# DeltaNet encoder kernel, opening of the first layer: gate products between the turns of the input, one convolution ahead of running sums, block norms one step later

## The reference, cut to what matters

```python
h = x @ w_in
qkv, z, b, a = jnp.split(h, [...])
qkv = jax.nn.silu(_short_conv(qkv, conv_w))      # 5 taps along the tokens, channel by channel
q, k, v = ...                                    # q and k l2-normalised
beta = jax.nn.sigmoid(b)
g = -jnp.exp(a_log) * jax.nn.softplus(a + dt_bias)
for d in range(2):                               # forwards and backwards in time
    g = jnp.cumsum(g, axis=-1)                   # inside a chunk of 64 tokens
    decay = jnp.exp(jnp.where(lower, g[..., :, None] - g[..., None, :], -jnp.inf))
    a = jnp.where(strict, jnp.einsum('nbhcd,nbhsd->nbhcs', k_beta, k) * decay, 0.0)
    t_inv = lax.linalg.triangular_solve(a + eye, ...)
    ...                                          # a scan over the chunks with a state
```

## Time and profile before

| | us |
|---|---|
| median of 3 runs | 1366.97 (1364.73 to 1369.42) |
| profiled execution, its own time | 1367.56 |
| its span in the trace | 1365.8 |
| TensorE busy, weight loads | 1309.2, 752.3 |
| VectorE busy | 791.1 |
| ScalarE busy | 351.4 |
| GpSimd busy | 304.1 |

### The profile page before, as it was taken

How to read it: one execution, slowest core, us unless ns; L and a number is a source line. 1 busy time by engine, 2 the same in 40 slices (tenths; PEclk the granted TensorE clock), 3 DMA queues, 4 the chain that set the end, 5 groups by cost and what they waited for, 6 DMA issues and landing times. The chain is left out here.

```text
span 1365.8 us, 22496 instructions
## 1 busy us (share of the span) xinstructions
PE 1309.2 (96%) x8070; PEld 752.3 (55%) x8070; DVE 791.1 (58%) x1733; ACT 351.4 (26%) x785; POOL 304.1 (22%) x536
## 2 busy tenths in 40 slices
PE   8999999999999999999998999999999998899995
PEld 5467575766757667586764333355455454533332
DVE  2857776676776766765675442284353546644227
ACT  3322323222222222222221222113422322122210
POOL 2263425052340523406012000220000000200025
PEclk9999999999999999999999999999999999899998
DMA  6440605225052250532426999840211138399972
GB/s 213 133 111 8 169 7 162 66 73 158 6 165 64 74 156 6 158 128 73 162 101 229 393 413 412 319 134 1 89 45 33 38 106 323 127 390 413 413 290 109
DMA packets 173207, 220.97 MB, mean 162 GB/s; under 512 B 57360, under 2 KB 107920, under 8 KB 173136
## 3 DMA queue, kind: packets, MB, share of 16 engines
q1 hardware_dynamic: 134736, 167.10, 35.3%
q10 hardware_dynamic: 33312, 34.87, 7.6%
q0 software_dynamic: 5088, 18.02, 3.7%
HBM read 185.63 MB, written 34.34 MB: 161 GB/s over the span
## 5 line engine op out<-in xcount | busy, mean ns | idle before, releaser
L531 PE MATMUL bank<-xT,wgu 128*128 128x512 f32 x448 | 197.8, 596 | 3.0 <-DVE wgu L1236 2.8
L2080 PE MATMUL bank<-wgu,moe_xgT 128*32 128x512 f32 x1536 | 169.8, 594 | 1.0 <-issue 0.7
L531 PEld LDWEIGHTS bank<-xT,wgu 128*128 128x128 f32 x448 | 84.2, 192 | 101.2 <-issue 101.0
L1236 DVE SCALAR_TENSOR_TENSOR wgu<-bank,taps,wgu 128x510 f32<-128x510 f32 (+1 forms) x128 | 95.6, 748 | 62.7 <-ACT wgu L833 56.9
L617 PE MATMUL bank<-wd,xT 128*128 128x256 f32 x512 | 118.9, 383 | 0.3 <-DVE res L1329 0.3
L2080 PEld LDWEIGHTS bank<-wgu,moe_xgT 128*32 128x32 f32 x1536 | 49.1, 110 | 103.5 <-issue 92.0
L583 PE MATMUL bank<-wd,oT 128*128 128x512 f32 x224 | 105.3, 593 | 0.0
L617 PEld LDWEIGHTS bank<-wd,xT 128*128 128x128 f32 x512 | 94.5, 190 | 16.3 <-issue 3.2
L2115 PE MATMUL bank<-wd,moe_hidT 128*32 128x512 f32 x768 | 87.0, 593 | 2.2 <-DVE moe_hidT L2365 1.2
L2361 DVE TENSOR_TENSOR moe_hid<-moe_silu,bank 128x256 f32<-128x256 f32 x24 | 10.1, 421 | 126.7 <-ACT moe_silu L2204 126.7
L1676 POOL DMA_INDIRECT wgu<-slots_y,fetch x8 | 11.4, 1427 | 273.6 <-DMA slots_y<-moe_y_rows 259.4
(11 more groups left out here) (359 smaller groups left out, 2285.0 us busy)
## 6 DMA issues: line engine op xcount, KB each, us to landing
wgu<-moe_w_gate SPq DMA_DIRECT2D x32, 1024.0 KB, 12.7
wgu<-moe_w_up SPq DMA_DIRECT2D x32, 1024.0 KB, 14.4
wd<-moe_w_down SPq DMA_DIRECT2D x32, 1024.0 KB, 15.2
wgu<-dn_w_in SPq DMA_DIRECT2D x32, 512.0 KB, 4.1
slots_x<-gains SPq DMA_DIRECT2D x5, 1920.0 KB, 10.3
xT<-slots_x ACTq DMA_DIRECT2D x16, 512.0 KB, 8.1
wgu<-gate_rows SPq DMA_DIRECT2D x14, 512.0 KB, 4.9
wd<-dn_w_out ACTq DMA_DIRECT2D x14, 512.0 KB, 4.3
```

The costliest lines, as they stand in the source:

```text
L531: mm = pe.matmul(bank[:], wqkv[:, ct, k], xT[:, k], start=k == 0, stop=k == KD - 1)
L1236: ins = nc.vector.scalar_tensor_tensor(out=conv[:, ct, lo:hi], in0=bank[:, lo + d:hi + d], scalar=w[:, j:j + 1], in1=conv[:, ct, lo:hi], o ...
L2080: mm = pe.matmul(ps[2][seats].rearrange("p (a f) -> p a f", a=2), xgT[:, j % ROW_BUFS, k, seats], wgu[:, e % RING, :, k], start=k == 0, st ...
```

## The change

There are three edits.

1. The load of `wba` leaves SyncE's list, where it stood behind x, and becomes ScalarE's first instruction. The gate products are cut by token tile: those of tile 0 stand behind the turns of tile 1, those of tile 1 behind the turns of tile 2, those of tiles 2 and 3 behind the turns of tile 3.
2. In the window ahead of the first body, VectorE's four scans of head 1 and `invert_norms(0)` move behind the first channel tile's taps, and change places with each other: the norms now come first.
3. In the body FIRST, and only there, `invert_norms(1)` moves from behind step 0 to behind step 1.

```diff
--- before.py
+++ after.py
@@ -384,7 +384,6 @@
             sp.dma_start(ident, dram["const"][:, C_ID:C_ID + P]).then_inc(ident_in, 16)
             for tt in range(TT):
                 sp.dma_start(res[:, tt], x_dram[:, tt]).then_inc(t["x_in"][tt], 16)
-            sp.dma_start(wba[:], w_dram[:, :, BA_OFF:BA_OFF + 4 * NV]).then_inc(ba_in, 16)
             sp.dma_start(c[:, C_ONE:C_ROW], dram["const"][:, C_ONE:C_ROW]).then_inc(small_in, 16)
             sp.dma_start(bvec[:, 0], dram["dn_a_log"][0].rearrange("d h -> (d h)").partition_broadcast(P)).then_inc(small_in, 16)
             sp.dma_start(bvec[:, 1], dram["dn_dt_bias"][0].rearrange("d h -> (d h)").partition_broadcast(P)).then_inc(small_in, 16)
@@ -504,6 +503,16 @@
                 mm.then_inc(full[uses.at[name][0]], 1)
 
             pe.wait_ge(ident_in, 16)
+            def gates_of(tt):
+
+                if tt == 0:
+                    pe.wait_ge(ba_in, 16)
+                pe.wait_ge(xT_ready, 2 * tt + 2)
+                for k in range(KD):
+                    mm = pe.matmul(ps[2][:, tt * 64:(tt + 1) * 64], xT[:, k, tt * P:(tt + 1) * P], wba[:, k], start=k == 0, stop=k == KD - 1)
+                if tt == TT - 1:
+                    mm.then_inc(full[2], 1)
+
             for n in range(8):
                 tt, half = n // 2, n % 2
                 if half == 0:
@@ -514,13 +523,9 @@
                 for k in range(4):
                     mm = pe.transpose(ps[b][:, k * P:(k + 1) * P], res[:, tt, (half * 4 + k) * P:(half * 4 + k + 1) * P], ident)
                 mm.then_inc(full[b], 1)
-
-            pe.wait_ge(ba_in, 16)
-            pe.wait_ge(xT_ready, 8)
-            for tt in range(TT):
-                for k in range(KD):
-                    mm = pe.matmul(ps[2][:, tt * 64:(tt + 1) * 64], xT[:, k, tt * P:(tt + 1) * P], wba[:, k], start=k == 0, stop=k == KD - 1)
-            mm.then_inc(full[2], 1)
+                if tt and half:
+                    gates_of(tt - 1)
+            gates_of(TT - 1)
 
             def project(uses, i, n, ct, part=(0, KD)):
                 if part[0] == 0:
@@ -798,6 +803,7 @@
                 act.wait_ge(full[b], n + 1)
                 return ps[b]
 
+            act.dma_start(wba[:], w_dram[:, :, BA_OFF:BA_OFF + 4 * NV]).then_inc(ba_in, 16)
             act.sem_inc(oT_ready, 1)
             for n in range(8):
                 b = 4 + n % 2
@@ -1308,13 +1314,14 @@
                         span(n, h, d)
 
             def window(uses, i, n):
-                if uses is not FIRST:
+                if uses is MAIN:
                     spans_of(n)
-                if uses is FIRST_HEAD:
-                    invert_norms(0)
                 for ct in range(3):
                     for tap in taps_apart(uses, i, n, ct):
                         tap()
+                    if uses is FIRST_HEAD and ct == 0:
+                        invert_norms(0)
+                        spans_of(n)
                     if ct:
                         silu(n, ct - 1)
                     if uses is FIRST and ct == 1:
@@ -1458,7 +1465,7 @@
                         else:
                             ins = nc.vector.tensor_tensor(flat, flat, bank[:, 0:256], ALU.add)
                         ins.then_inc(o_step, 1)
-                    if st == 0 and following:
+                    if following and st == (0 if earlier else 1):
                         invert_norms(i + 1)
                     if earlier and st < 3 and add_then[st] is not None:
                         add_output("y", add_then[st])
```

## The result

| | before | after |
|---|---|---|
| median | 1366.81 us (4 runs, 1364.73 to 1369.42) | 1374.72 us (4 runs, 1374.03 to 1375.58) |
| ratio, 95% interval | | 1.0052 (1.0032 to 1.0072) |
| profiled execution, its own time | 1367.56 us | 1374.71 us |
| span | 1365.8 us | 1372.9 us |

The change makes the kernel slower by about 7.9 us, 0.5%. The forecast was 1370.7 with a range up to 1374. A second measurement (the last experiment) gave 1.0042 (1.0028 to 1.0056), so the sign is certain and the two intervals together allow 4 to 10 us.

The account below looks back on a forecast made before the run. TensorE, busy 1309 of 1366 us, was taken as the bound. Terms -1.7 + 1.9 + 1.0 + 1.4 + 1.1 = +3.7 us on 1367.6, with the median 0.6 lower: 1370.7, range 1364 to 1374.

Parts of the forecast that it names:

- edit 1, projection's start: Opening: gate products between the turns start the projection earlier, -1.7 us, ends -2.1 and -0.7.
- edit 2 at V, without the opening: Head 1's window: late solve and placing loads move the mask and V product by +1.9 us, ends -1.8 and +2.6.
- half clock behind it: TensorE at half rate behind new stands: +1.0 us behind the one at 89.7, +1.1 before head 2's projection.
- edit 3 at head 2's projection: Later norms delay the solve, GpSimd's roots and the taps, so head 2's projection moves by +1.4 us.
- later stages: After 150 us: a shift at 150 us was counted as a shift of the end, so 0 more.
- The solve's four operations: GpSimd beside head 1's scans: each operation waits for a scan, so the fourth ends at 73.4, 3.2 us late.
- The stand behind z: TensorE after the first half of z, from 89.7 until the placed blocks land: at least 2.3 us, about 3.4.
- Rival A: The solve isn't held: small operations slip between the scans, or share; 1364.4 us, chance 0.20.
- rival C: The solve's lateness is absorbed by slack and all stalls are gained, 8.7 us: 1358.3 us, chance 0.09.
- Rival D: Opening: `wba` lands late and the first gate products hold the turns, edit 1 gives nothing: 1372.4 us, chance 0.06.
- rival B: Half rate decides: both new stands bring a long stretch, each 3.4 us: +8.4, 1375.4 us, chance 0.15.

Follow-up runs that it names:

- the last experiment: The changed kernel measured again, beside the two others on the same chip, against the kernel before: 1374.28 us, ratio 1.0042.
- the sums split: Second edit with two of head 1's sums ahead of the norms, two behind its last convolution: 1363.80 us with norms behind `r`, 1366.52 us without that move.
- the cut sums: Second edit alone on the kernel before, with head 1's four running sums over one column instead of 512: 1371.86 us.
- the norms behind `r` alone: Kernel before, with head 1's block norms moved behind VectorE's `r` of step 1, ahead of that step's outputs: 1365.50 us, ratio 0.9976.
- both edits in their other form: Kernel before, plus two sums before and two after the solve, middle tap ahead of placing loads, norms behind `r`, no first edit: 1363.80 us, ratio 0.9973.
- the second alone: Kernel before, with two sums ahead of the norms, two behind the last convolution, middle tap ahead of placing loads, head 1's norms unmoved: 1366.52 us, ratio 0.9987.
- three products in the stand: Changed kernel, with three dummy TensorE products ahead of its wait for head 1's placed blocks: 1374.83 us, ratio 1.0043 to the kernel before.
- its load moved: First edit alone on the kernel before, gate weights issued by SyncE behind the second tile of x: 1365.86 us, ratio 0.9986.

## Why the prediction was right or wrong, step by step

| step | forecast | measured (profiled execution) |
|---|---|---|
| edit 1, projection's start | -1.7 | -0.52; mean over 5 executions about +0.2 against 7 without it |
| edit 2 at V, without the opening | +1.9 | +1.6 |
| half clock behind it | +1.0 | +2.0 |
| edit 3 at head 2's projection | +1.4 | +0.9 |
| half clock behind it | +1.1 | +1.6 |
| later stages | 0 | +1.6 |
| sum | +3.7 | +7.1 |

**The waits were right.** Both mechanisms by which the change loses were forecast, with their places. The solve's four operations were to end 3.2 us late by the sums: they take 5.87 us where the undisturbed ones take 2.75 (67.27 to 70.02 with the sums split), so 3.1. The placing loads were to move by 3.7 us: 2.93 + 0.52 of the opening = 3.45. The third tile was to wait 1.3 us: 1.44. The stand behind z was to be about 3.4 us: 3.07. The norms of the third edit were to be done at 124.5 on the old clock, 3.3 late: 127.37 + 0.25 less the +3.07 is 124.55. The wait of 4 us or more before head 2's projection came as two, 0.87 and 2.45 us, 3.3 together. Rival A, that the solve isn't held, is out by the cut sums; rival C, that all stalls are gained, too. The Trainium skill (SBUF — State Buffer, Who interferes with whom) has a VectorE instruction with two SBUF inputs and a GpSimd instruction that reads SBUF contend for ports that are held as an exclusive lock, and the trace agrees, down to the small operation that took 0.91 us instead of 0.21.

**Edit 1 failed on a step that I hadn't seen.** I took the gate products at the pace of the earlier trace rows, 7.22 us for 64 records, wherever they stood. In the gaps between the turns they cost up to twice that, as the turns themselves do, and the delay of x was 1.0 us (5.92 against 4.91) instead of 0.7. My estimate from the Trainium skill's 512 B for line rate (DMA: Bandwidth & Descriptors, Specifications) was a delay of 1.4 us; the measured 1.0 lies between it and mine by bytes. But the load isn't the main cause: with it out of the way the projection still started at 19.97. The five executions range from 18.59 to 21.45, so a gain of half a microsecond on average isn't excluded; one of 1.7 doesn't fit them. Rival D named the result, not the reason: the weights landed at 4.6 us, well in time.

**The clock was mis-sized.** I took 1.0 and 1.1 us for half rate, below the 1.6 us of a full stretch on dense work, because I thought the work behind V wasn't dense and because a wait of 2 us before brought none. The first stretch came double (6.8 us, 2.0 lost), the second whole (1.6 lost). That lies a third of the way to rival B, which had a price of 3.4 for each (3.6 lost together, 2.1 forecast, 6.8 in B). My upper bound of 1.7 was too low for the first, since a stretch of 6.8 us was in the earlier trace rows already, behind another stand.

**A shift at 150 us isn't the shift of the end.** I said that I count it so. It was +5.5 at 160 and +7.1 at the end; the rest came in later stages that no edit touches, most of it about the stands and stretches of half clock in the second layer. In the repeat the shift was 4.8 at 197 us, 6.0 at 1197 and 7.8 at 1276, the last part by a stand of 1.87 us at 1201 and half clock behind it. The second edit alone kept its shift (+2.9 at 122 us, +3.0 at the end), the third went from +1.6 at 197 us to +2.6. What sets these later differences stays open; I made no run for it.

**The size against the range.** The sum lacks 3.4 us: 1.2 by edit 1, 1.0 and 0.5 by the clock, 1.6 from later, less 0.8 by which the waits were milder. The +1.5 for edit 3 among the upper ends has no working; by its own paragraph it is 1.4. I forecast slower by 0.3% and called it no change; the measured 0.5% is past that bound, and 0.7 us past the end of the range, which held no price for stretches of half clock in later stages.

## What to carry to other kernels

Before you move work into a gap of one engine, look at who else is released by it: here the norms start a chain on GpSimd, and sums with two SBUF inputs behind the norms hold that chain for longer than the stall that was removed. Put such operations where the other engine is idle or waiting, and put a wait behind what others are waiting for rather than a whole step later (the norms behind `r` alone made the kernel 0.24% faster). Price a new stand of TensorE with the half clock that may follow it, and price products that fill gaps at the rate of that place, not at the rate that they had elsewhere.

## What the runs showed of the hardware

- Stands of the same length bring half clock in one execution and not in another. 2.80 us at 69 us: none with the first edit alone, 3.4 us behind 2.82 to 2.93 in four other executions. Two stands of about 1.6 and 1.3 us around the X products: 3.4 us with both edits in their other form, none with the second alone. Both stretches of the change, 6.8 and 3.4 us, came again in the repeat. Every stand of 3.07 to 3.12 us had one, of 6.8 us in three executions and of 3.4 in one.
- A stand's end doesn't set where half clock begins. In the repeat it began at 91.93, before the X products at 92.38. In all seven executions that had it there, it began 81.9 us behind the first entry of the trace's list of granted clocks (92.63 less 10.71 in the change, 97.74 less 15.82 with three products in the stand), while the X products began 78.9 to 82.4 us behind that entry. So where a stand lies against the opening's step may decide beside its length; no run tests that.
- The opening's matmul records are long at first (0.42 us each, 0.28 later), and the step falls between 8.1 and 15.8 us. Back to back they start 0.21 us apart before it and 0.11 behind it, so the pace about doubles. The views give the granted clock as 1.00 over both, but the trace's list of granted clocks has no entry before the step: its first, at full clock, is at 8.67 us before the change, 10.71 after it, 15.53 with the first edit alone and 14.02 with its load moved, and within 0.2 us of the step in all 13 traces. So the slow records are most likely half clock that has no record.
- An instruction on VectorE is held as well as holding. The sums took 1.69 and 1.68 us beside the solve instead of 1.2, a `silu` beside GpSimd's decayed scores (L1103) 1.76 instead of 0.68, and a sum beside GpSimd's addition of sums (L1024) 2.28 instead of 1.19.
